# First block's gate and up by seven quarter products; the modulation rows shared out anew

## What is computed

```python
D_MODEL = 1024; SEQ = 128; DEC_SEQ = 512; DEPTH = 2; D_FF = 2816
def modulation(cond, w_mod, b_mod):
    m = jax.nn.silu(cond) @ w_mod + b_mod          # 1024 x 6144 per layer
    return jnp.split(m[..., None, :], 6, axis=-1)
def swiglu(h, w_gate, w_up, w_down):
    return (jax.nn.silu(h @ w_gate) * (h @ w_up)) @ w_down
for l in range(DEPTH):
    ...                                            # mixer, gated residual
    hp = rms_norm(xp, norm_ffn[l]) * (1.0 + sc2_c) + sh2_c
    hs = rms_norm(xs, norm_ffn[l]) * (1.0 + sc2_s) + sh2_s
    xp = xp + g2_c * swiglu(hp, ffn_w_gate[l], ffn_w_up[l], ffn_w_down[l])
    xs = xs + g2_s * swiglu(hs, ffn_w_gate[l], ffn_w_up[l], ffn_w_down[l])
```

## Time and profile before

| | |
|---|---|
| Timed runs | 1569.66, 1569.92, 1566.68 us (median 1569.66) |
| Profiled execution | span 1566.4 us from first to last instruction; no time of its own is given beside the span, which is 0.3 us under the fastest timed run and 3.2 us under the median |
| TensorE busy | 1538.6 us, 98% of the span, 10775 matmuls |
| VectorE, ScalarE, GpSimd busy | 71%, 47%, 18% |
| Mean granted TensorE clock | 0.995 of 2.4 GHz |
| Layer 0's FFN | 384.9 to 860.4 us |
| Layer 1's FFN | 1119.8 us to the end |

### The profile page before, as it was taken

One profiled execution on the slowest core, in us unless ns is written; L12 is line 12 of the kernel. 1 busy time (PEld: TensorE's weight loads), 2 busy tenths in 40 slices (PEclk: granted clock), 3 DMA queues, 4 the chain that ended last, 5 costly groups with the idle time before them and its releaser, 6 DMA issues.

```text
span 1566.4 us, 26496 instructions
## 1 busy us (share of the span) xinstructions
PE 1538.6 (98%) x10775; PEld 1483.5 (95%) x10775; DVE 1113.9 (71%) x1882; ACT 743.6 (47%) x1236; POOL 287.6 (18%) x344
## 2 busy tenths in 40 slices
PE   8989999999999999999999999999999999999998
PEld 6989788899999999999999899989999999999998
DVE  5657877866779746665467999988688468568453
ACT  3435555653544423442235766676365335335332
POOL 0010111000156524453253023221000000000000
PEclk9999999999999999999999999999999999999999
DMA  9332332132354544444333388875203222222322
GB/s 329 110 109 62 110 103 82 36 122 81 96 168 148 162 128 127 155 136 135 113 116 95 78 180 174 175 151 132 81 28 101 88 81 75 88 81 75 91 68 78
DMA packets 142464, 178.12 MB, mean 114 GB/s; under 512 B 13025, under 2 KB 121257, under 8 KB 141320
## 3 DMA queue, kind: packets, MB, share of 16 engines
q1 hardware_dynamic: 120128, 109.68, 22.3%
q0 software_dynamic: 21888, 66.66, 17.2%
q10 hardware_dynamic: 328, 0.10, 0.0%
HBM read 148.93 MB, written 2.79 MB: 97 GB/s over the span
## 4 chain that ended last, share of the span: by engine, by line
PE 87%; DVE 8%; ACT 2%; issue 1%; DMA 1%; POOL 0%; DVEq 0%; ACTq 0%
PE PS L777 23%; PE PS L779 22%; PE PS L782 22%; PE PS L858 5%; PE PS L860 5%; PE PS L859 5%; PE PS L1185 1%; PE PS L1196 1%; PE PS L1138 1%; DVE PTL L2698 1%; DMA MODA<-in_w_mod 1%; DVE WL L2099 0%; PE PS L1161 0%; DVE TMP L2288 0%; DVE X L2441 0%
## 5 line engine op out<-in xcount | busy, mean ns | idle before, releaser
L777 PE MATMUL PS<-HH,WH 128*128 128x320 f32 (+1 forms) x1168 | 269.6, 312 | 2.8 <-DVE HL L2299 2.2
L779 PE MATMUL PS<-HL,WH 128*128 128x320 f32 (+1 forms) x1168 | 266.1, 309 | 0.0
L782 PE MATMUL PS<-HH,WL 128*128 128x320 f32 (+1 forms) x1168 | 265.4, 308 | 0.0
L2425 DVE SCALAR_TENSOR_TENSOR X<-PS,MODV,X 128x128 f32<-128x128 f32 (+2 forms) x216 | 81.6, 434 | 185.4 <-PE PS L782 185.3
L777 PEld LDWEIGHTS PS<-HH,WH 128*128 128x128 f32 x1168 | 194.5, 188 | 7.5 <-issue 3.5
L779 PEld LDWEIGHTS PS<-HL,WH 128*128 128x128 f32 x1168 | 196.0, 188 | 0.0
L782 PEld LDWEIGHTS PS<-HH,WL 128*128 128x128 f32 x1168 | 195.8, 188 | 0.0
L2099 DVE TENSOR_TENSOR WL<-RAW,WH 128x2048 fp32r<-128x2048 f32 (+2 forms) x56 | 126.6, 2261 | 65.1 <-ACT WH L1503 64.9
L777 PE MATMUL PS<-HIDH,WH 128*128 128x320 f32 x704 | 163.0, 312 | 0.3 <-DVE HIDL L2356 0.3
L1867 ACT ACTIVATE BGW<-BGW,SC 128x512 f32<-128x512 f32 x112 | 80.8, 723 | 173.4 <-DVE BGACC L2247 124.0
L699 POOL TENSOR_TENSOR BGACC<-BGACC,BGW 128x512 f32<-128x512 f32 x97 | 132.4, 1365 | 159.8 <-ACT BGW L1867 158.6
(11 more groups left out here) (409 smaller groups left out, 3206.0 us busy)
## 6 DMA issues: line engine op xcount, KB each, us to landing
BGW<-in_w_mod POOLq DMA_DIRECT2D x112, 256.0 KB, 3.0
RAW<-in_ffn_w_gate SPq DMA_DIRECT2D x22, 1024.0 KB, 5.3
RAW<-in_ffn_w_up SPq DMA_DIRECT2D x22, 1024.0 KB, 5.4
MODA<-in_w_mod POOLq DMA_DIRECT2D x48, 256.0 KB, 3.7
RAW<-in_ffn_w_down SPq DMA_DIRECT2D x16, 768.0 KB, 4.7
RAW<-in_ffn_w_down SPq DMA_DIRECT2D x8, 1024.0 KB, 5.1
RAW<-in_conv_w_pw SPq DMA_DIRECT2D x16, 512.0 KB, 5.3
WL<-RAW POOLq DMA_DIRECT2D x8, 1024.0 KB, 9.8
```

Of the source, the lines that this page charges most:

```text
L777: mm(o, wh, xh, start=first, stop=False)
L779: mm(o, wh, xl, start=False, stop=False)
L782: ins = mm(o, wl, xh, start=False, stop=last)
L2425: ins = V.scalar_tensor_tensor(out=X[:, m, t:t + b - a], in0=tile2(n)[:, bank, a:b], scalar=g, in1=X[:, m, t:t + b - a], op0=ALU.mult, op1 ...
```

## The change

- `FAST_FROM` is 2 for both layers, and `DOWN_K` is 6, 6, 6, 4 for both: layer 0 takes the quarter products too, with the same ring, sums and copies. The ring is laid out for both layers, and in layer 0 the last down step's blocks start three places further (`RING_GAP`).
- The 14 halves are shared out anew. Eight of them (the keys are layer and pair) are multiplied on TensorE inside a gate unit, after its first and after its sixth quarter product, into the second bank of a PSUM tile in use, and picked in the up unit. GpSimd only loads their pieces (four buffers MODB).
- The other six halves are three parts of 1024 columns. Each is done in one of layer 0's down steps 0 to 2: VectorE multiplies and adds all eight rows for the first condition and the rows 4 to 7 for the second; ScalarE scales the rows 0 to 3 for the second, and transfers that add collect them in BGACC. VectorE merges both at the end of the step, turns and sums the first condition there, and the second behind the next gate unit. TensorE picks the part in the up unit of that pair (8, 14 and 20). The row buffers lie where TMP and ACTV lie, so ScalarE's copies wait until they are free.
- The work on halves leaves the pair steps, the last down step and the convolution's start; the last LayerNorm's `last_half_sum` becomes eight more clock-holding matmuls.

```diff
-DOWN_K = ((8, 8, 6), (6, 6, 6, 4))
+DOWN_K = ((6, 6, 6, 4), (6, 6, 6, 4))
-FAST_FROM = (1, 2)
+FAST_FROM = 2
+RING_GAP = 3
+PE_HALVES = {(0, 4): 0, (0, 6): 1, (0, 10): 8, (0, 12): 9, (0, 16): 10, (0, 18): 11, (1, 4): 12, (1, 6): 13}
+PART_AFTER = (8, 14, 20)
+BG_BY_DMA = 4
+BG_AT = ((), (0, 1), (2,), (3,), (4,), (5,), (6,), (7,))
...
+                def between(i):
+                    if turn is not None and i == 3:
+                        turn_half_rows(tile2(n2), turn)
+                    if part is not None and i == 3:
+                        part_sums(tile2(n2), part)
+                    if rows is not None and i in (0, 5):
+                        half_rows(tile2(n2), rows, i // 5)
...
+            def half_rows(ps, j, step):
+                for g in range(GROUPS):
+                    k = GROUPS * step + g
+                    i = KT * PE_ORDER.index(j) + k
+                    if g == 0:
+                        pe.wait_ge(sem("modb_landed"), 16 * (i + GROUPS))
+                    ins = mm(ps[COLG * g:COLG * (g + 1), 1, :], SC[:, k, :], MODB[i % MOD_SLOTS][:], start=(step == 0), stop=(step == 1))
+                ins.then_inc(sem("modb_used"), 1)
...
+            def part_rows(q):
+                pool.wait_ge(sem("hid_ready"), PART_AFTER[q])
+                for k in range(3):
+                    part_load(q, k)
+                for k in range(BG_BY_DMA):
+                    pool.wait_ge(sem("bgw_scaled"), BG_STEPS * q + k + 1)
+                    for h in range(2 if k else 0):
+                        c = slice(512 * h, 512 * (h + 1))
+                        if k > 1:
+                            part_added(q, k - 1, h)
+                        pool.dma_start(BGACC[1][:, c], BGW[k % 3][:, c], accum_op=ALU.add).then_inc(bgw_added[h], 16)
+                    if k == 0:
+                        part_load(q, 3)
+                    elif k > 1:
+                        part_load(q, k + 2)
+                part_added(q, BG_BY_DMA - 1, 0)
+                part_added(q, BG_BY_DMA - 1, 1)
+                part_load(q, 6)
+                pool.wait_ge(sem("bgw_scaled"), BG_STEPS * q + 6)
+                part_load(q, 7)
...
+            def part_turned(q, s):
+                if s:
+                    dve.wait_ge(sem("bgw_scaled"), BG_STEPS * (q + 1))
+                else:
+                    dve.wait_ge(sem("bgw_first"), KT * (q + 1))
+                    dve.wait_ge(sem("half_summed"), PE_BEFORE[q])
+                for h in range(2):
+                    link(V.transpose(BGTURN[:].rearrange("p i g c -> p (i g c)"), BGACC[s][:, 512 * h:512 * (h + 1)]))
+                    ins = V.tensor_reduce(out=BGSUM[:, s, 4 * h:4 * h + 4, :], in_=BGTURN[:], op=ALU.add, axis=mybir.AxisListType.X)
...
                     residual(name(m), m, l, which)
+                    if chunk is not None and l == 0 and not norm_name:
+                        for k in BG_AT[m]:
+                            part_first(chunk, k)
+                            if k >= BG_BY_DMA:
+                                part_second(chunk, k)
+                        if m == KT - 1:
+                            part_merged(chunk)
+                            part_turned(chunk, 0)
...
-                if l == FAST_FROM[0]:
-                    whole_apply(n, l, 1)
-                else:
-                    apply(n, l, 1)
+                whole_apply(n, l, 1)
...
-            last_half_sum()
-            hold_clock(tile2(("mh", N_HALF - 1)), 2)
+            spare = begin(("pw2", 0))
+            hold_clock(spare, 10)
```

More of the change, by code:

```diff
@@ L390, in program @@
         REC8 = small("REC8", [P, QT])
+        BGTURN = sb("BGTURN", [P, 4, GROUPS, COLG], R_BG + 4096)
+        BGSUM = small("BGSUM", [P, 2, KT, GROUPS])
+        MODB = [sb(f"MODB{i}", [P, 512], R_ROOT + 2048 * i) for i in range(MOD_SLOTS - 1)] + [sb("MODB3", [P, 512], R_BG)]
+        BGACC = [sb("BGACC0", [P, D], R_ROOT), sb("BGACC1", [P, D], R_BG)]
+        BGW = [sb(f"BGW{i}", [P, D], R_MOD + 2 * quarter + 4096 * i) for i in range(3)]
+        assert R_MOD + 2 * quarter + 3 * 4096 <= R_T[6]
         assert top[0] <= nc.sbuf_usable_end
@@ L530, in program, with ringed, layer, fast @@
         moved = [U[("glu", LOW_BY_DMA)] <= u < U[("glu", LOW_BY_DMA)] + KT for u in range(len(units))]
+        RING_AT = [U[("up", l, FAST_FROM)] for l in range(2)]
+        RING_END = [U[("glu", 0)], len(units)]
+        def ringed(u):
+            return any(a <= u < b for a, b in zip(RING_AT, RING_END))
+        def layer(u):
+            return 0 if u < RING_END[0] else 1
+        def fast(u):
+            return ringed(u) and units[u][0][0] in ("gate", "up")
+        BLK, FASTN, GATES, UPS, nblk = {}, {}, {}, {}, 0
+        for u in range(len(units)):
+            if not ringed(u):
+                continue
+            BLK[u] = nblk
+            nblk += FAST if fast(u) else units[u][1] // BLOCK
+            if fast(u):
+                FASTN[u] = len(FASTN)
+                GATES[u] = sum(units[v][0][0] == "gate" for v in FASTN if v < u)
+                UPS[u] = sum(units[v][0][0] == "up" for v in FASTN if v < u)
+        block_unit = [u for u in BLK for _ in range(FAST if fast(u) else units[u][1] // BLOCK)]
+        last_chunk = BLK[U[("down", 0, len(DOWN_K[0]) - 1, 0)]]
+        slot, place = [], 0
+        for b, u in enumerate(block_unit):
+            if b == BLK[RING_AT[layer(u)]]:
+                place = RING_AT[layer(u)] % 2 * RING // 2
+            if b == last_chunk:
+                place += RING_GAP
+            slot.append(place % RING)
+            place += 1
+        def before(b):
+            first = BLK[RING_AT[layer(block_unit[b])]]
+            return max((a for a in range(first, b) if slot[a] == slot[b]), default=None)
+        def unit_freed(eng, u):
+            if RING_END[0] <= u < RING_END[0] + 2:
+                block_used(eng, max(b for b in range(BLK[RING_AT[1]]) if slot[b] // (RING // 2) == u % 2))
+            elif u >= 2:
+                filled(eng, unit_last[u - 2])
+        def plain_before(u):
+            return sum(not ringed(v) for v in range(u + 1))
         def low_there(eng, u):
[L534 to L535 removed]
+            if ringed(u):
+                eng.wait_ge(sem("block_low"), BLK[u] + (FAST if fast(u) else units[u][1] // BLOCK))
             elif moved[u]:
@@ new lines, in _, with half_loads @@
+            filled(pool, ("rb", "ffn0"))
+            def half_loads(first, last):
+                for i in range(KT * first, KT * last):
+                    r, k = divmod(i, KT)
+                    if i >= MOD_SLOTS:
+                        pool.wait_ge(sem("modb_used"), (i - MOD_SLOTS) // GROUPS + 1)
+                    l, c0 = divmod(FIRST_BG * D + PE_ORDER[r] * 512, 6 * D)
+                    pool.dma_start(MODB[i % MOD_SLOTS][:], w_mod[l, k * P:(k + 1) * P, c0:c0 + 512]).then_inc(sem("modb_landed"), 16)
@@ L2364, in fast_posts @@
                 up = kind == "up"
+                rows, turn, part = bg_half(l, kind, a), bg_turn(l, kind, a), bg_part(l, kind, a)
                 dst = TMP if up else ACTV
@@ L2399, in fast_posts @@
                         hidden_low(l, a + j, j)
-                low_blocks(b + 7 + lead)
+                if rows is not None:
+                    turn_half(rows, ps2)
+                low_blocks(u, b + 7 + lead)
+                if l == 0 and not up and a in PART_AFTER:
+                    part_turned(PART_AFTER.index(a), 1)
             def apply(norm_name, l, half, midway=None):
```

522 lines of the change are left out of this document (249 added, 273 removed).

## The result

The changed kernel takes 1589.4 us (median of four runs, 1581.8 to 1591.9) against 1569.6 us for the kernel before: ratio 1.0121, 95% interval 1.0095 to 1.0146. It is slower by 1.2%. The prediction was 1571.6 with a range up to 1586, so the time lies outside. The profiled execution has a span of 1590.1 us, 23.7 more than before, where the prediction had 1.9 more. It is the slowest of the four. The mean granted clock was 0.995 in the execution of 1581.8 us and 0.986 to 0.989 in the other three, so a good part of the loss comes and goes with stretches at the lower clock.

The account below looks back on a forecast made before the run. TensorE, busy for 98% of the span, was taken as the bound. Terms -34.0 - 4.7 - 3.2 + 5.4 + 15.9 + 4.0 + 12.9 + 2.1 + 3.5 = +1.9 us gave about 1571.6 us, range 1556 to 1586.

Parts of the forecast that it names:

- With 3.9 each reload lands 1 to 5 us before its turn: Down steps 0 to 2: at 3.9 us per pair of adding transfers, row buffers are reloaded before VectorE needs them.
- T+8.0: VectorE reaches the next gate unit's low parts 8.0 us after T, the end of the down step's last matmul.
- chunk ends: Behind down steps 0 to 2, VectorE's row work delays each gate 4.3 us (+12.9) and each up unit 0.7 (+2.1).
- The mechanism was among the rivals: Slow adding transfers in down steps 0 to 2 make VectorE stand still: +24 us, 1596 in all, chance 0.12.
- the nearer row: For adding-transfer time, the ZACC row's 3.9 us for a 256 KB pair was preferred to the Y row's 8.8.
- Quarter products, -34.0; entry, +5.4: Layer 0: 19 units go from 96 to 84 matmuls, saving 34.0 us; getting into the scheme costs 5.4.
- Half rows, +15.9; picks, +4.0: Eight halves on TensorE: 16 steps of 1.14 us, less 2.3 in existing waits; eleven picks of 0.36 us.
- rival 3: Half rows' transfers are late: up to 1 us for each of 16 TensorE steps, 1580 in all, chance 0.12.
- Small prices on VectorE: Row work in down steps: multiply-add of 1024 columns 1.27 us, merge about 1.22, one condition's turn 3.0.
- Ring's gap, +3.5: Last down step's blocks three places further: late roundings delay three products in one unit, +3.5 us (0 to 4).
- Rival 1: Down steps' row work is hidden because the next gate unit has more lead: 1556.6 us, chance 0.2.
- rival 4: Small prices too high: gap covered, no slow stretches, smoother first quarter units; up to -8 us, 1564, chance 0.18.

Follow-up runs that it names:

- the run with one step of two: Only the second of each half's two TensorE steps kept, on the kernel with rows 1 to 7 on VectorE (1574.2 us): 1575.7 us, ratio 1.0039.
- Two experiments that shorten the transfers' part in different ways: On the changed kernel: adding transfers cut to 32 of 512 columns, 1574.5 us; rows 1 to 7 on VectorE with no adding transfers, 1574.2 us.

## Why the prediction was wrong

The step that failed is "With 3.9 each reload lands 1 to 5 us before its turn", and with it the T+8.0 at which VectorE was to come to the gate. In the term's own words, the chunk ends, +12.9 and +2.1, measured 32.6. The chunk ends were priced for a VectorE that is on time at T; it was 4.9 us behind, because the reload of row 5 stood behind two pairs of adding transfers and beside 1 MB of weights, and landed after 9.0 us, 4.66 too late. The mechanism was among the rivals, with its threshold ("From about 6 us on VectorE stands still") and at a chance of 0.12; the adding transfers took 5.7 in the median and 8.2 beside the weights, between the two rows that I weighed. I took the nearer row because "one or two in flight" described the ZACC transfers; the load that SyncE issues at 526.99 I had not laid beside them. By the fit that the Trainium skill gives in "DMA: Bandwidth & Descriptors", section "Anatomy of one DMA — SWDGE (gpsimd) path", about 2.0 us plus the bytes at 436 GB/s, such a transfer would take an estimated 2.6 us; the adding transfers of this trace, at 4.3 to 8.3 us, don't agree with it.

Point by point:
- *Quarter products, -34.0; entry, +5.4*: right. Seven products stream in 12.3 us, the second block's stretch of 73.7 is the same, and gate 4 shows the waits of 1.8 and 1.1 us. With the row work out, the rest of the sum gives 1555.5, and 1560.9 with the 5.4 us of the last down step that it lacks; measured were 1559.9.
- *Half rows, +15.9; picks, +4.0*: right. What such a piece costs is what it adds between the products around it. From 474.57 to 476.05 there are 1.48 us for two products (0.29) and a step of four, so 1.19 against 1.14 counted; from 467.18 to 467.85 there are 0.67 for two products and a pick, so 0.38 against 0.36. The distance from the piece's own first matmul to the next product, 1.00 and 0.18 us, leaves out the delay ahead of it and behind it; the expectation of the run with one step of two reckoned with it. No wait for MODB stands in the changed kernel's table: rival 3 fell.

```profile
467.18 0.31 PE L842 MATMUL PS<-T1H,WL 128*128 128x320 f32 x1
467.42 0.25 PE L901 MATMUL PS<-BGTURN,PICK 128*32 128x8 f32 x8
467.60 0.41 PE L840 MATMUL PS<-HH,WH 128*128 128x320 f32 x1
467.85 0.31 PE L841 MATMUL PS<-HL,WH 128*128 128x320 f32 x1
...
474.57 0.30 PE L842 MATMUL PS<-HH,WL 128*128 128x320 f32 x1
474.80 1.07 PE L895 MATMUL PS<-MODB,SC 128*32 128x512 f32 x8
475.80 0.42 PE L840 MATMUL PS<-HH,WH 128*128 128x320 f32 x1
476.05 0.31 PE L841 MATMUL PS<-HL,WH 128*128 128x320 f32 x1
```

- *Small prices on VectorE*: right. A multiply-add over 1024 took 1.28 us, the merge 1.22, transpose and reduction over 512 0.71 and 0.69. The chain from VectorE's return to the copy of P is 4.7 + 0.4 us, 5.1 forecast.
- *Chunk ends, +12.9 and +2.1*: right for a VectorE on time (4.4 a gate without the adding transfers, 13.3 in all), 17.6 us short for this kernel, and this is the term that was mis-sized. In the three windows TensorE is idle for 20.6 us, 6 more than the 14.4 I had, and loses some 10.6 by running slow, where I had put 0.6. Two experiments that shorten the transfers' part in different ways took 15 us off, and with them most of the slow stretches. The slow part varies from one execution to the next, as the one of 1581.8 us shows.
- *Ring's gap, +3.5*: right for the up unit (3.7 with the late pick), but the gap also makes the wait for HIDL in the last down step, 5.4 us with the slow stretch behind it. I had called that step hidden.
- *Rival 1* (hidden after all) fell; *rival 4* fell too: the small prices were right, the gap cost what was put down for it, and slow stretches there were.

What stays open: whether the 5.4 us of the last down step can be had without the wait that the gap avoids, and why the clock falls behind the same waits in one kernel and not in another, or in one execution and not in the next.

## What to carry to other kernels

When background work shares an in-order engine with the work that feeds TensorE, ask where its engine will be when the stage ends, and take the time of its transfers with all that the other queues issue in the same few microseconds, not alone. Then look for what is tied to it by queue order alone: moving one copy ahead of a rounding that it doesn't need was worth 5 to 8 us here, and starting the background work in the engine's idle time at the beginning of the stage, without the chained transfers, turned a loss of 20 us into a gain of 3. Buffers that share space are waits too: list who else uses the bytes before moving work into them.

## What the runs showed of the hardware

In the first down step adding transfers of 256 KB took 4.3 to 8.3 us, the slow ones beside a load of 1 MB that itself took 9.2 us, against 5.1 to 5.5 for the loads of that size right behind the first two down steps; a 512 KB load issued behind them took 9.0, where the median was 4.8. A group of four matmuls of 512 columns on 32-column groups added 1.19 us between products of 320 columns, and a pick of 8 columns 0.38. Taking 0.8 us of matmuls out of each of eight places left the waits behind the down steps as they were and brought a granted clock of 0.93 in three windows that had shown 1.00.
